# Strassen's scheme for four of the eleven chunks of each down projection of a four-layer transformer kernel

## The reference

```python
def swiglu(x, w_gate, w_up, w_down):
    return (jax.nn.silu(x @ w_gate) * (x @ w_up)) @ w_down
```

## Time and profile before

| | |
|---|---|
| median of 3 runs | 1249.65 us (1249.41 to 1251.18) |
| span of the profiled execution | 1248.4 us (its own time outside the span isn't recorded) |
| PE busy | 1236.7 us, 99%, 6366 matmuls and transposes |
| DVE busy | 811.4 us, 65% |
| ACT busy | 668.3 us, 54% |
| granted TensorE clock | 1.000 |
| the chain that ended last | PE 93% |

### The profile page before, as it was taken

One profiled execution on the slowest core, in us unless ns is written; L12 is line 12 of the kernel. 1 busy time (PEld: TensorE's weight loads), 2 busy tenths in 40 slices (PEclk: granted clock), 3 DMA queues, 4 the chain that ended last, 5 costly groups with the idle time before them and its releaser, 6 DMA issues.

```text
span 1248.4 us, 15780 instructions
## 1 busy us (share of the span) xinstructions
PE 1236.7 (99%) x6366; PEld 1031.4 (83%) x6366; DVE 811.4 (65%) x1037; ACT 668.3 (54%) x965; POOL 89.2 (7%) x121
## 2 busy tenths in 40 slices
PE   7999999999999999999999999999999999999998
PEld 6778888888888888888888888888888888888887
DVE  7995756654788766554687746656547785655553
ACT  7865653433898654443687535444436644544431
POOL 2410000000100100000232000000001300000000
PEclk9999999999999999999999999999999999999999
DMA  7344555555554565555554235555555315555551
GB/s 306 105 140 144 190 198 172 199 173 199 189 200 163 192 222 183 192 179 200 181 199 169 68 102 169 202 192 179 184 192 181 131 39 202 199 186 185 183 188 67
DMA packets 32536, 216.60 MB, mean 173 GB/s; under 512 B 3904, under 2 KB 4544, under 8 KB 7376
## 3 DMA queue, kind: packets, MB, share of 16 engines
q1 hardware_dynamic: 30384, 210.32, 48.8%
q0 software_dynamic: 1360, 4.78, 1.2%
q10 hardware_dynamic: 720, 0.50, 0.1%
HBM read 214.54 MB, written 1.05 MB: 173 GB/s over the span
## 4 chain that ended last, share of the span: by engine, by line
PE 93%; DVE 4%; issue 1%; DMA 1%; ACT 0%; SPq 0%; DVEq 0%; ACTq 0%
PE PS L461 26%; PE PS L463 26%; PE PS L462 26%; PE PS L467 6%; PE PS L791 2%; PE PS L815 1%; PE PS L496 1%; PE PS L498 1%; PE PS L495 1%; PE PS L544 1%; PE PS L538 1%; PE PS L539 1%; DVE WL L1748 1%; DMA X<-in_x 1%; DVE YG L2037 1%
## 5 line engine op out<-in xcount | busy, mean ns | idle before, releaser
L1748 DVE TENSOR_TENSOR WL<-RAW,WH 128x2048 fp32r<-128x2048 f32 (+2 forms) x200 | 442.9, 2218 | 310.6 <-ACT WH L1130 310.6
L1130 ACT ACTIVATE WH<-RAW 128x2048 fp32r<-128x2048 f32 (+2 forms) x200 | 371.2, 1858 | 366.4 <-PE PS L463 366.1
L461 PE MATMUL PS<-WH,HTh 128*128 128x512 f32 (+1 forms) x848 | 334.6, 395 | 0.2
L463 PE MATMUL PS<-WH,HTl 128*128 128x512 f32 (+1 forms) x848 | 329.0, 388 | 0.0
L462 PE MATMUL PS<-WL,HTh 128*128 128x512 f32 (+1 forms) x848 | 328.3, 387 | 0.0
L463 PEld LDWEIGHTS PS<-WH,HTl 128*128 128x128 f32 x848 | 159.2, 188 | 33.2
L461 PEld LDWEIGHTS PS<-WH,HTh 128*128 128x128 f32 x848 | 159.4, 188 | 32.0 <-DVE WL L1748 0.8
L462 PEld LDWEIGHTS PS<-WL,HTh 128*128 128x128 f32 x848 | 159.5, 188 | 30.6
L461 PE MATMUL PS<-WH,YAh 128*128 128x512 f32 x402 | 158.6, 394 | 0.1
L463 PE MATMUL PS<-WH,YAl 128*128 128x512 f32 x402 | 156.7, 390 | 0.0
L462 PE MATMUL PS<-WL,YAh 128*128 128x512 f32 x402 | 156.5, 389 | 0.0
(11 more groups left out here) (354 smaller groups left out, 1442.9 us busy)
## 6 DMA issues: line engine op xcount, KB each, us to landing
RAW<-in_w SPq DMA_DIRECT2D x196, 1024.0 KB, 4.9
BC<-in_rows POOLq DMA_DIRECT2D x4, 512.0 KB, 4.0
YG<-in_mem POOLq DMA_DIRECT2D x4, 512.0 KB, 4.7
X<-in_x SPq DMA_DIRECT2D x2, 512.0 KB, 5.4
RAW<-in_w SPq DMA_DIRECT2D x4, 256.0 KB, 6.0
BC<-in_s SPq DMA_DIRECT2D x1, 512.0 KB, 11.6
YG<-in_s SPq DMA_DIRECT2D x1, 512.0 KB, 11.9
BB<-in_s SPq DMA_DIRECT2D x1, 512.0 KB, 12.5
```

Of the source, the lines that this page charges most:

```text
L461: e.matmul(out, ah, bh, start=start, stop=False)
L463: return e.matmul(out, al, bh, start=False, stop=stop)
L1130: e.activation(WH[:, c % NW, w], RAW[:, c % NR, w], ACT.Copy).then_inc(S.hi, 1)
L1748: e.tensor_tensor(WL[:, c % NW, w], RAW[:, c % NR, w], WH[:, c % NW, w].bitcast(f32), SUB).then_inc(S.lo, 1)
```

## The change

Chunks 2, 4, 6 and 8 of each down projection (`FAST`) are done by Winograd's form of Strassen's scheme. With the activations' blocks Y(k, t) and the weights' blocks B, seven products stand for eight: three with single weight blocks, W(1) to W(3), and four (T(0) to T(3)) with sums of weight blocks. The first block isn't split any more (`piece`: columns 512 to 2047).

- VectorE forms four sums of weight blocks from `RAW` into `TR_` (the buffer `YG`), ScalarE their high parts (`sums_hi`, into `HTh`), VectorE the remainders (`sums_lo`, into `HTl`).
- The sums of activation blocks are formed at fold 2, 4, 6 and 8 (`form_sums`, five 128x128 operations, between two copies of ScalarE), and split with one more operation on each engine.
- Four products go to banks of their own (4 to 7), accumulated over the four chunks. During and after chunk 8 eight additions of VectorE (`combine`) bring them together in banks 0 to 3, on which the tail then accumulates.
- Chunk 2 waits for fold 10, whose bank 4 it reuses.

```diff
+FAST = (2, 4, 6, 8)
+NF = len(FAST)
...
+        if ci in FAST:
+            out.append([cut(down, lead, k, 1, [(512, 512)]), cut(down, lead, k, 1, [(0, 512)]), cut(down, lead, k + 1, 1, [(0, 1024)])])
...
+                TS = sb(key + "TS", [128, 4, 512])
+                TH, SG = (TS[:, 2 * i:2 * i + 2, :].rearrange("p a (t c) -> p a t c", t=2) for i in range(2))
+                out = [YBh, YBl, TH, SG, sb(key + "AN", [128, 2, 2, 256]), TS]
+                out += [sb(key + n, [128, NF, 384], f32r) for n in ("SFh", "SFl")]
...
+        FASTS = {PLAN[FFNS[f]][22 + ci]: NF * f + i for f in range(4) for i, ci in enumerate(FAST)}
+        T_ORDER = (1, 0, 2, 3)
+        TSh, TSl = (a[:, :, :].rearrange("p (n a) c -> p n (a c)", a=2) for a in (HTh, HTl))
+        SR = JK[:, :].rearrange("p (b c) -> p b c", b=2)
+        TR_ = YG[:, :, :].rearrange("p a (b c) -> p (a b) c", b=2)
...
+            def fast_chunk(f, ci, c):
+                i, m = FAST.index(ci), FASTS[c]
+                hi, lo, j = ydst(f, 2 * ci)
+                SFh, SFl = FB[f][6:8]
+                W = lambda n: (WH[:, c % NW, 512 * n:512 * n + 512], WL[:, c % NW, 512 * n:512 * n + 512])
+                T = lambda n: (TSh[:, n, :], TSl[:, n, :])
+                Y = lambda k, t: (hi[:, j + k, 128 * t:128 * t + 128], lo[:, j + k, 128 * t:128 * t + 128])
+                S_ = lambda n: (SFh[:, i, 128 * n:128 * n + 128], SFl[:, i, 128 * n:128 * n + 128])
+                def mul(b, a, w, own):
+                    return mm3(PS[:, b, :], *a, *w, own and i == 0, i == NF - 1)
+                e.wait_ge(S.lo, c + 4)
+                tk = mul(5, Y(0, 0), W(1), True)
+                if i == NF - 1:
+                    tk.then_inc(S.ms, 1)
+                e.wait_ge(S.tlo, 4 * m + 1)
+                mul(6, S_(0), T(1), True).then_inc(S.tu, 1)
+                e.wait_ge(S.tlo, 4 * m + 2)
+                mul(4, Y(0, 1), T(0), True).then_inc(S.tu, 1)
+                for b, a, w in ((0, Y(1, 0), W(2)), (1, S_(2), W(3))):
+                    tk = mul(b, a, w, False)
+                    if i == NF - 1:
+                        tk.then_inc(S.ms, 1)
+                e.wait_ge(S.tlo, 4 * m + 3)
+                mul(7, S_(1), T(2), True).then_inc(S.tu, 1)
+                e.wait_ge(S.tlo, 4 * m + 4)
+                mul(2, Y(1, 1), T(3), False).then_inc(S.used, 1)
...
+                        if f is not None and i == 0:
+                            e.wait_ge(S.cb, 8 * f + 4 * t + 4)
...
-                wide_mm(cs[22:], ed + 1, lambda k: ydst(f, k), lambda ci: e.wait_ge(S.ylo, fold_n(f, ci)), lambda: fold(10), 1)
+                wide_mm(cs[22:], ed + 1, lambda k: ydst(f, k), lambda ci: e.wait_ge(S.ylo, fold_n(f, 10 if ci == FAST[0] else ci)), lambda: fold(10), 1, f)
...
+            def sums_hi(c):
+                m = FASTS[c]
+                e.wait_ge(S.used, c - 1)
+                for q, n in enumerate(T_ORDER):
+                    e.wait_ge(S.tr, 4 * m + (2, 3, 3, 4)[q])
+                    copy(TSh[:, n, :], TR_[:, n, :]).then_inc(S.thi, 1)
...
+                    if f is not None and ci == FAST[-1]:
+                        e.wait_ge(S.ms, 3 * f + 1)
+                        copy(FB[f][5][:, 0, :], PS[:, 5, :]).then_inc(S.eo, 1)
                     feed(c)
+                    if f is not None and ci + 2 in FAST:
+                        sums_hi(cs[ci + 2])
...
+                    if g in FAST:
+                        n = FAST.index(g)
+                        e.wait_ge(S.fold, fold_n(f, g))
+                        copy(SR[:, g % 2, 384:512], PS[:, 4 + g % 2, 128:256]).then_inc(S.sa, 1)
+                        e.wait_ge(S.sr, 3 * (NF * f + n) + 3)
+                        copy(hi[:, j:j + 2, :], pair(4 + g % 2), 0.5)
+                        copy(FB[f][6][:, n, :], SR[:, g % 2, 0:384], 0.5).then_inc(S.yhi, 1)
...
+            def sums(c):
+                m = FASTS[c]
+                B12, B11, B21, B22 = (RAW[:, c % NR, 512 * n:512 * n + 512] for n in range(4))
+                if m:
+                    e.wait_ge(S.tlo, 4 * m)
+                e.tensor_tensor(TR_[:, 2, :], B22, B12, SUB).then_inc(S.tr, 1)
+                e.wait_ge(S.tr, 4 * m + 1)
+                e.tensor_tensor(TR_[:, 1, :], TR_[:, 2, :], B11, ADD).then_inc(S.tr, 1)
+                e.tensor_tensor(TR_[:, 0, :], B12, B11, SUB).then_inc(S.tr, 1)
+                e.wait_ge(S.tr, 4 * m + 2)
+                e.tensor_tensor(TR_[:, 3, :], B21, TR_[:, 1, :], SUB).then_inc(S.tr, 1)
...
+            def sums_lo(c):
+                m = FASTS[c]
+                for q, n in enumerate(T_ORDER):
+                    e.wait_ge(S.thi, 4 * m + q + 1)
+                    rest(TSl[:, n, :], TR_[:, n, :], TSh[:, n, :]).then_inc(S.tlo, 1)
...
+            def combine(f, c):
+                m, cb = FASTS[c], 8 * f
+                E1, U, V, Q = (FB[f][5][:, n, :] for n in range(4))
+                def join(out, b, a, after=0):
+                    if after:
+                        e.wait_ge(S.cb, cb + after)
+                    e.tensor_tensor(out, PS[:, b, :], a, ADD).then_inc(S.cb, 1)
+                e.wait_ge(S.eo, f + 1)
+                e.wait_ge(S.tu, 3 * m + 1)
+                join(U, 6, E1)
+                e.wait_ge(S.tu, 3 * m + 2)
+                join(V, 4, U, 1)
+                e.wait_ge(S.ms, 3 * f + 2)
+                join(PS[:, 0, :], 0, E1)
+                e.wait_ge(S.ms, 3 * f + 3)
+                join(PS[:, 1, :], 1, V, 2)
+                e.wait_ge(S.tu, 3 * m + 3)
+                join(Q, 7, U)
+                join(E1, 7, V, 3)
+                join(PS[:, 3, :], 3, E1, 6)
+                e.wait_ge(S.used, c + 1)
+                join(PS[:, 2, :], 2, Q, 5)
...
+                    if f is not None and ci == 0:
+                        sums(cs[FAST[0]])
+                    if f is not None and ci == FAST[-1]:
+                        combine(f, c)
                     feed(c)
+                    if f is not None and ci and ci + 3 in FAST:
+                        sums(cs[ci + 3])
+                    if f is not None and ci + 2 in FAST:
+                        sums_lo(cs[ci + 2])
...
+                if c - NR in FASTS:
+                    e.wait_ge(S.tr, 4 * FASTS[c - NR] + 4)
```

More of the change, by code:

```diff
@@ L34, in ffn_chunks @@
             out.append([("pair", gate, up, lead, k, 4, 256 * g, uo + 256 * g)])
-    return out + wide(down, lead, 22)
+    for ci in range(11):
+        k = 2 * ci
+        if ci in FAST:
+            out.append([cut(down, lead, k, 1, [(512, 512)]), cut(down, lead, k, 1, [(0, 512)]), cut(down, lead, k + 1, 1, [(0, 1024)])])
+        else:
+            out.append([cut(down, lead, k, 2, [(0, 1024)])])
+    return out
 def plan():
@@ L459, in pe, with mm3 @@
         def pe(e):
[L460 to L463, removed]
+            def mm3(out, ah, al, bh, bl, start, stop, joined=False):
+                e.matmul(out, ah, bh, start=start, stop=False, skip_group_check=joined)
+                e.matmul(out, ah, bl, start=False, stop=False, skip_group_check=joined)
+                return e.matmul(out, al, bh, start=False, stop=stop, skip_group_check=joined)
             def transp(out, src):
@@ L582, in rows_mm, with wide_mm @@
                         hook(ci)
-            def wide_mm(cs, ed, src_of, before, behind=None, at=0):
-                n = len(cs)
+            def fast_chunk(f, ci, c):
[24 more added lines that the diff above has]
+                mul(2, Y(1, 1), T(3), False).then_inc(S.used, 1)
+            def wide_mm(cs, ed, src_of, before, behind=None, at=0, f=None):
+                n, fast = len(cs), f is not None
                 def both(c, k, t):
@@ L590, in both @@
                         o = (k % 2) * 1024 + half * 512
-                        tk = product(c, PS[:, 2 * t + half, :], (hi, lo), j, t, slice(o, o + 512), k == 0, k == 2 * n - 1)
+                        tk = product(c, PS[:, 2 * t + half, :], (hi, lo), j, t, slice(o, o + 512), k == 0,
+                                     k == 2 * n - 1 or fast and t == 1 and half == 1 and k == 2 * FAST[-1] - 1, fast and k > 2 * FAST[-1])
                     return tk
                 for ci, c in enumerate(cs[:-2]):
+                    if c in FASTS:
+                        before(ci)
+                        fast_chunk(f, ci, c)
+                        continue
                     e.wait_ge(S.lo, c + 4)
@@ L1811, in rows_mm, with wide_mm @@
                         hook(ci)
-            def wide_mm(cs, ed, behind=None, after=(), at=0):
+            def sums(c):
[36 more added lines that the diff above has]
+                join(PS[:, 2, :], 2, Q, 5)
+            def wide_mm(cs, ed, behind=None, after=(), at=0, f=None):
                 for ci, c in enumerate(cs[:-2]):
@@ L1874, in ffn @@
                         beside(g)
-                wide_mm(cs[22:], ed + 1, lambda: fold(10), at=1)
+                wide_mm(cs[22:], ed + 1, lambda: fold(10), at=1, f=f)
             def mem_lo(i):
```

41 lines of the change are left out of this document (32 added, 9 removed).

## The result

The changed kernel takes **1263.24 us** (median of four runs, 1261.91 to 1263.85), the kernel before 1249.53 beside it (1249.20 to 1251.18). The ratio is 1.0103, with a 95% interval of 1.0089 to 1.0116: 1% slower. The forecast was 1257.3 in a range of 1252 to 1265: right sign, inside the range, 5.9 us short. The profiled execution took 1263.05 us; its span is 1261.2.

What follows compares the result with a forecast made beforehand. The prediction took TensorE, 99% busy, as the bound. It summed -10.9 us for fewer matmuls, +8.7 for waits ahead of chunk 2 and +9.8 for waits at the joins to +7.6, giving 1257.3 us, range 1252 to 1265.

Steps and rivals of the forecast that it cites:

- Bound and saving: TensorE, 99% busy, bounds the kernel; 21 matmuls for 24 in each changed down-projection chunk take 10.9 us off.
- 48 x 0.227: Matmuls removed over four chunks in four layers, times the 0.227 us spacing read from chunk 1: 10.9 us saved.
- First gap: Ahead of chunk 2, TensorE waits for fold 10's remainder, queued behind VectorE's block sums: 2.17 us a layer, 8.7 in all.
- Second gap: Between chunk 8 and the tail, TensorE waits for four joins behind chunk 10's remainder: 2.45 us a layer, 9.8 in all.
- Steady chunks and gate phase: Changed chunks' splits and sums, and the activation sums at folds, stay covered by 1.0 and 1.4 us: no cost.
- Rival D: VectorE operations don't overlap, adding 1.1 us a layer at hand-overs ahead of chunk 2 and the joins: 1261.7, chance 0.01.
- Rival C: TensorE's clock falls to 1.2 GHz at the eight gaps, 2 to 4 us each: 1273 to 1289 us, chance 0.04.
- the two waits: Sign: new TensorE waits, four times each, about 1.9 us for fold 10's remainder and about 2.3 us for a join.
- the 48 matmuls: Sign: TensorE should issue 48 fewer matmuls, at a spacing of 0.227 us.
- the joins' price: Sign: VectorE's joins, writing into PSUM, should take 0.69 us each.
- the granted clock of 1.00: Sign: TensorE's matmuls should run at a granted clock of 1.00.
- Rival A: VectorE arrives before TensorE waits: at joins and chunk 2, 1238.8 us, chance 0.05; at joins alone, 1247.5, chance 0.05.

Runs made afterwards that it cites:

- the kernel with both edits: Changed kernel with four joins ahead of chunk 10's weight remainder and chunk 2 waiting for fold 10 only before its last product, into bank 4: 1240.22 us.
- Joins-first kernel: Changed kernel with VectorE's first four joins and ScalarE's copy of bank 5 moved ahead of chunk 10's remainder and conversion: 1248.86 us.
- Kernel with dummies: Changed kernel with eight unused matmuls into bank 5 in each layer, just ahead of the tail's wait for the joins: 1258.28 us.
- the four waits of 4.02 us: Waits ahead of chunk 2 in the changed kernel with two unused VectorE reductions of 128x1024 ahead of fold 10's remainder: 1275.95 us.
- the kernel with the 2.37 us waits: Changed kernel with one unused VectorE subtraction of 128x512 ahead of fold 10's remainder, lengthening the wait ahead of chunk 2: 1267.01 us.

## Why the prediction was right in direction and short in size

- **Bound and saving.** Right: TensorE bounds, and each matmul is worth its spacing and not its duration. The saving, forecast at 10.9 us, is 9.8 in the kernel with both edits (1240.22 beside 1250.03, 7.6 to 11.8 by the interval, so the times alone don't tell the two apart). The missing 1.1 us fits the spacing of the changed chunks in the trace: 336 matmuls by 0.004 to 0.005 us are 1.3 to 1.7. The term "48 x 0.227" took the spacing of the other chunks for these.
- **First gap.** Forecast 2.17 us a layer, 8.7 in all. Timeline: 2.01. Joins-first kernel less the one with both edits: 1248.86 - 1240.22 = 8.6. The queue came as listed. The changed kernel is 0.61 us ahead here, and with that taken off the forecast had the sums from 257.37 (measured 257.36) and fold 10 at 264.66 (264.50). The 0.16 is spacing: independent operations of 512 columns start 0.60 apart and not 0.62.
- **Second gap.** Forecast 2.45 a layer, 9.8 in all. Timeline: 2.40 and 0.11 of restart (the forecast had 0.09 in it). Kernel with dummies less joins-first: 1258.28 - 1248.86 = 9.4. Joins into PSUM are two in 1.29 us, 0.69 each, the nearest row's value.
- **Steady chunks and gate phase.** Right at nothing. No matmul of a changed chunk waits in the list, and from layer 0's first fold to its last 113.47 us pass before (150.02 to 263.49) and after (149.41 to 262.88).
- **Rival D** (VectorE operations that don't overlap) is out: four remainders still take 2.49 us, and every sum but the one that needs the one before starts 0.60 to 0.61 after it. The section that the prediction cites against this, of the Trainium skill ("VectorE: DVE Perf Modes", section "The DRAIN you can't avoid"), says also that an operation which is not held starts earlier, so these rows contradict its first sentence but not the section as a whole.
- **Rival C is what failed.** It had a chance of 0.04, because "gaps of 2.2 and 2.5 us have no example", and that lack was used as evidence against it. It speaks for neither side; the only gap of length in the trace of before, 5.0 us at the start, had slow matmuls behind it. It was also priced as all or nothing, eight gaps by 2 to 4 us. It came in part: three in eight, 1.54 us each, 4.6 in all (5.0 by the kernel with the dummies). A chance per gap belonged in the sum; with the measured three in eight it gives 1257.3 + 4.6 = 1261.9.

Sum from the runs: -9.8 + 8.6 + 9.4 + 5.0 = +13.2 against +13.7 measured. This shares the total out and doesn't prove it, since each difference begins where the last ends. The timeline gives it from other numbers: -10.9 + 1.5 (spacing) + 8.0 (first gaps) + 10.0 (second gaps) + 4.6 (three set backs) = +13.2. Forecast, with neither the spacing nor the set backs: +7.6.

That 1263.24 lies inside 1252 to 1265 is in part luck. The upper end came from joins into PSUM at 1.2 us and a VectorE queue 0.8 us longer ahead of chunk 2; the joins took 0.69 and the queue was 0.16 us shorter. What filled that room was the clock, which the range left out. Of the signs named, the two waits (1.77 for about 1.9, 2.24 for about 2.3), the 48 matmuls and the joins' price came; the granted clock of 1.00 did not (0.996).

Rival A's reasons stand too: nothing in the changed kernel gets VectorE there first. But with the joins moved ahead in VectorE's queue, and TensorE's product for bank 4 put last, neither wait is there, and the kernel is at 1240.2, beside the 1238.8 of that rival.

## What to carry to other kernels

When TensorE is 99% busy, fewer matmuls pay only if the work that replaces them comes in time. Ask of each new wait what stands ahead of its releaser in that engine's queue and what the waiting engine could do first, and move that before giving up the idea: here order alone turned 1% slower into 0.8% faster. Price a new gap of about 2 us in TensorE at its length plus a share of the clock's set back behind it.

## What the runs showed of the hardware that was not expected

- A set back costs the same behind the one gap of 1.77 us as behind those of 2.24: 7 or 8 matmuls of 512 columns at 0.43 apart instead of 0.23, 1.5 to 1.6 us. Behind 4.02 us it was up to 13 matmuls and 2.5 us.
- The clock does not fall at a fixed point of a gap. It fell 1.3 us after work went on again (1.77 us wait), just at the gap's end (2.24, layer 0 of the changed kernel; in layer 2, behind the same wait, 0.6 us after it), and behind the four waits of 4.02 us once 1.3 us before the end, once 1.2, once 0.3, and once 0.9 us after it.
- Idle time in one piece is not the only way. In the kernel with the 2.37 us waits seven matmuls from 65.13 on were slow too, behind waits of 0.56 and 0.61 us and a run of small matmuls (32x128); the granted clock of 60 to 66 us was 0.91. The other kernels, the changed one too, have the same small matmuls and such waits (0.81 and 0.60 us in the changed one) with no slow matmul behind them.
- The clock's column doesn't show everything: it has 1.00 for the first 20 us of the kernel before, where matmuls of 512 columns start 0.42 apart.
- The same fp32r matmul of 512 columns starts 0.227 us after the last in most chunks and 0.232 in the changed ones. The cause is open.
- Eight useless matmuls in each second gap, 32 in all, made the kernel 5.0 us faster.
